# One decoder layer on one Trainium2 core: the last chunk's value and gate tiles taken by pairs of rows at the seam between feed-forward and mixer

## What is computed

```python
x = x + 0.5 * rmsnorm(swiglu_ffn(rmsnorm(x, ffn1_pre_g), ffn1_w_gu, ffn1_w_down), ffn1_post_g)
# mixer
u = rmsnorm(x, mix_pre_g) @ w_in
u_val, u_glu, u_x, u_gelu = jnp.split(u, [D_CONV, 2 * D_CONV, 2 * D_CONV + D_LRU], axis=-1)
g = u_val * sigmoid(u_glu)                       # "value" and "gate" of the conv branch
c = silu(rmsnorm(causal_dwconv([conv_buf | g], conv_w, conv_b), conv_norm_g))
yb = rg_lru(causal_dwconv([lconv_buf | u_x])) * gelu(u_gelu)
x = x + rmsnorm(concat(c, yb) @ w_out, mix_post_g)
# second feed-forward half step, gated per-layer embedding
```

## Time and profile before

| | |
|---|---|
| median of 3 runs | 2153.56 us (2152.64 to 2153.91) |
| profiled execution | 2149.13 us |
| its span, first to last instruction | 2147.0 us |
| mean granted TensorE clock | 0.99 |
| PE busy | 2084.6 us, 97% |
| DVE busy | 1189.7 us, 55% |
| ACT busy | 684.9 us, 32% |
| POOL busy | 70.0 us, 3% |

### The profile page before, as it was taken

How to read it: one execution, slowest core, us unless ns; L and a number is a source line. 1 busy time by engine, 2 the same in 40 slices (tenths; PEclk the granted TensorE clock), 3 DMA queues, 4 the chain that set the end, 5 groups by cost and what they waited for, 6 DMA issues and landing times. The chain is left out here.

```text
span 2147.0 us, 34634 instructions
## 1 busy us (share of the span) xinstructions
PE 2084.6 (97%) x13116; PEld 2071.4 (96%) x13116; DVE 1189.7 (55%) x2368; ACT 684.9 (32%) x1403; POOL 70.0 (3%) x109
## 2 busy tenths in 40 slices
PE   7999999999999998999989999999999999999998
PEld 7999999999999998999979999999999999999998
DVE  5643545344543578447765764354534454367877
ACT  4321222212122234216774542111221212123555
POOL 0000000000000001330000000000000000000000
PEclk9999999999999999999999999999999999999999
DMA  5170111011101100332121311011101110011212
GB/s 163 60 115 23 59 59 59 10 49 59 59 23 36 59 20 25 75 65 40 40 70 51 98 57 43 19 59 59 59 10 49 59 59 27 32 59 45 75 40 101
DMA packets 153277, 116.17 MB, mean 54 GB/s; under 512 B 72648, under 2 KB 143628, under 8 KB 153200
## 3 DMA queue, kind: packets, MB, share of 16 engines
q1 hardware_dynamic: 117728, 108.41, 16.2%
q10 hardware_dynamic: 33424, 5.67, 1.9%
q0 software_dynamic: 2048, 1.06, 0.3%
HBM read 105.96 MB, written 9.15 MB: 54 GB/s over the span
## 5 line engine op out<-in xcount | busy, mean ns | idle before, releaser
L845 PE MATMUL ps<-x_hi,w_lo 128*128 128x352 f32 x2688 | 885.9, 330 | 13.9 <-DVE x_lo L2093 8.1
L847 PE MATMUL ps<-x_hi,w_hi 128*128 128x352 f32 x2688 | 871.3, 324 | 0.0
L846 PE MATMUL ps<-x_lo,w_hi 128*128 128x352 f32 x2688 | 867.0, 323 | 0.0
L845 PEld LDWEIGHTS ps<-x_hi,w_lo 128*128 128x128 f32 x2688 | 507.5, 189 | 16.4 <-DVE x_lo L2093 7.8
L846 PEld LDWEIGHTS ps<-x_lo,w_hi 128*128 128x128 f32 x2688 | 510.9, 190 | 0.0
L847 PEld LDWEIGHTS ps<-x_hi,w_hi 128*128 128x128 f32 x2688 | 508.0, 189 | 0.0
L845 PE MATMUL ps<-a_hi,wd_lo 128*128 128x352 f32 x1104 | 360.0, 326 | 9.2 <-DVE a_lo L2149 7.3
L847 PE MATMUL ps<-a_hi,wd_hi 128*128 128x352 f32 x1104 | 358.7, 325 | 0.0
L846 PE MATMUL ps<-a_lo,wd_hi 128*128 128x352 f32 x1104 | 356.8, 323 | 0.0
L2200 DVE TENSOR_TENSOR acc<-ps,acc 128x352 f32<-128x352 f32 x480 | 249.7, 522 | 91.0 <-PE ps L847 82.9
L2132 DVE TENSOR_TENSOR tmp_u<-ps,rstd_pre 128x352 f32<-128x352 f32 x132 | 69.0, 524 | 341.5 <-PE ps L847 341.5
(11 more groups left out here) (226 smaller groups left out, 1597.7 us busy)
## 6 DMA issues: line engine op xcount, KB each, us to landing
raw<-in_ffn_w_gu_dram SPq DMA_DIRECT2D x88, 512.0 KB, 3.5
rawd<-in_ffn_w_down_dram SPq DMA_DIRECT2D x22, 1024.0 KB, 7.9
raw<-in_w_in_dram SPq DMA_DIRECT2D x16, 512.0 KB, 4.6
raw<-in_w_out_dram SPq DMA_DIRECT2D x16, 512.0 KB, 3.5
raw<-in_ple_w_gate_dram SPq DMA_DIRECT2D x16, 512.0 KB, 3.6
toeplitz<-rev ACTq DMA_DIRECT2D x8, 512.0 KB, 8.3
x_in<-in_x_prompt_dram SPq DMA_DIRECT2D x4, 512.0 KB, 10.1
toep_first<-toeplitz SPq DMA_DIRECT2D x32, 64.0 KB, 2.3
```

The source lines that it names most:

```text
L845: eng.matmul(dst, wl, xh, start=first, stop=False)
L846: eng.matmul(dst, wh, xl, start=False, stop=False)
L847: return eng.matmul(dst, wh, xh, start=False, stop=last)
```

## The change

All of it lies at the seam between the first feed-forward half and the mixer.

1. TensorE, chunk 2: in place of two groups of eight rows each, the four tiles go pair of rows by pair of rows (`vg_part`): for q = 0 to 3, wait for `x_lo` of pair q, rows 2q and 2q+1 of tiles 0 and 1, then of tiles 2 and 3. `norm_sum("pre2", 2)` stands behind the whole.
2. TensorE, norms: `norm_sum("pre2", 1)` and `norm_spread("pre2", 1)` move from rows 0 and 1 of chunk 2 to rows 5 and 7 of chunk 1; `norm_spread("pre2", 2)` moves from row 1 to row 3 of `in_unit(2)`'s first tile.
3. TensorE, weights: the four uses of `in_unit` (units 2, 3, 6, 7) wait for the first half of their weights at row 0 and for the second at row 4 of the first tile.
4. VectorE: the `x_lo` of pair q of chunk 2 comes before the `post1_pair` of pair q+1, with one short block between (`glu_mults(0)`, `values(1)`, `glu_gates(1)`); the adds of squares of chunk 2 are moved back behind; `split_wide(mix + 2)` comes before `glu_mults(1)`.
5. ScalarE: the mean of ("pre2", 1) comes before pair (2, 0), its spread before pair (2, 1); in pairs 2 and 3 of chunk 2 `x_hi` goes ahead, and the squares 4 to 7 are spread over the places behind, two of them behind `glu_batch(1)`.

```diff
-            def tile_product(dst, s, t, c, mid=None, xs=(x_hi, x_lo)):
+            def tile_product(dst, s, t, c, mid=None, xs=(x_hi, x_lo), halves=None):
                 for k in range(KT):
+                    if halves is not None and k % 4 == 0:
+                        eng.wait_ge(wide_lo, halves + k // 4 + 1)
...
+            def vg_part(c, ns, q):
+                eng.wait_ge(x_lo_done, PAIRS * c + q + 1)
+                for n in ns:
+                    at = RING["vg", c, n]
+                    dst = bank(at) if q == 0 else ps[:, at % BANKS, 0:C]
+                    for k in (2 * q, 2 * q + 1):
+                        wh, wl = wide(n // 2, k, n % 2)
+                        mm = passes(dst, wh, wl, x_hi[:, k, cols(c)], x_lo[:, k, cols(c)],
+                                    k == 0, k == KT - 1)
+                    if q == PAIRS - 1:
+                        mm.then_inc(psum_full, 1)
             def second_norms(k):
-                if k == 0:
+                if k == 5:
                     norm_sum("pre2", 1)
-                if k == 1:
+                if k == 7:
                     norm_spread("pre2", 1)
-            def third_norms(k):
-                if k == 4:
-                    norm_sum("pre2", 2)
...
-            vg_group(1, (0, 1, 2, 3))
-            vg_group(2, (0, 1), second_norms)
-            vg_group(2, (2, 3), third_norms)
+            vg_group(1, (0, 1, 2, 3), second_norms)
+            for q in range(PAIRS):
+                vg_part(2, (0, 1), q)
+                vg_part(2, (2, 3), q)
+            norm_sum("pre2", 2)
...
             def in_unit(u, behind=None, mid=None):
-                eng.wait_ge(wide_lo, 2 * (WIDE0["mix"] + u + 1))
...
-                                 mid and (lambda k: mid(n, k)))
+                                 mid and (lambda k: mid(n, k)),
+                                 halves=2 * (WIDE0["mix"] + u) if n == 0 else None)
...
-                if (n, k) == (0, 1):
+                if (n, k) == (0, 3):
                     norm_spread("pre2", 2)
```

ScalarE:

```diff
             pre2_pair(1, 3)
+            mean("pre2", 1)
             pre2_pair(2, 0)
-            mean("pre2", 1)
+            spread("pre2", 1)
             pre2_pair(2, 1)
-            spread("pre2", 1)
-            pre2_pair(2, 2)
+            pair_hi(2, 0, acc_tile, 2)
+            pre2_square(4)
+            pair_hi(2, 0, acc_tile, 3)
+            pre2_square(5)
             glu_batch(1)
-            pre2_pair(2, 3)
+            pre2_square(6)
+            pre2_square(7)
             split_wide(WIDE0["mix"] + 2)
```

VectorE:

```diff
-            post1_pair(2, 0)
+            post1_pair(2, 0, ())
             glu_mults(0)
-            post1_pair(2, 1)
-            post1_pair(2, 2)
+            pair_x_lo(2, 0, acc_tile, 0)
+            post1_pair(2, 1, ())
             values(1)
+            add_square(NORM["pre2", 2], 1)
+            pair_x_lo(2, 0, acc_tile, 1)
+            post1_pair(2, 2, ())
             glu_gates(1)
-            post1_pair(2, 3)
+            pair_x_lo(2, 0, acc_tile, 2)
+            post1_pair(2, 3, ())
+            add_square(NORM["pre2", 2], 2)
+            add_square(NORM["pre2", 2], 3)
+            pair_x_lo(2, 0, acc_tile, 3)
+            for m in range(4, KT):
+                add_square(NORM["pre2", 2], m)
+            split_wide(WIDE0["mix"] + 2)
             glu_mults(1)
-            split_wide(WIDE0["mix"] + 2)
             values(2)
```

More of the change, by code:

```diff
@@ L1440, in squares, with pair_hi @@
                     square(i, m, src(m), sem_, count0 + m + 1)
-            def apply_pair(name, c, x0, src, q):
-                i = NORM[name, c]
+            def pair_hi(c, x0, src, q):
                 eng.wait_ge(x_new, x0 + PAIRS * c + q + 1)
@@ L1448, in apply_pair @@
                                ).then_inc(x_hi_done, 1)
+            def apply_pair(name, c, x0, src, q):
+                pair_hi(c, x0, src, q)
                 for m in (2 * q, 2 * q + 1):
-                    square(i, m, src(c, m)[:, 0, :])
+                    square(NORM[name, c], m, src(c, m)[:, 0, :])
             def silu(f, i, c, h):
@@ L1629, in pre2_pair, with pre2_square @@
                 apply_pair("pre2", c, 0, acc_tile, q)
+            def pre2_square(m):
+                square(NORM["pre2", 2], m, acc_tile(2, m)[:, 0, :])
             for m in range(KT):
@@ L2089, in bank_last, with pair_x_lo @@
                 return bank(n)
-            def pair_low(pre, c, x0, src, p):
+            def pair_x_lo(c, x0, src, p):
                 eng.wait_ge(x_hi_done, x0 + PAIRS * c + p + 1)
@@ L2095, in pair_low @@
                                   ).then_inc(x_lo_done, 1)
+            def pair_low(pre, c, x0, src, p):
+                pair_x_lo(c, x0, src, p)
                 for k in (2 * p, 2 * p + 1):
```

## The result

| | before | after |
|---|---|---|
| median | 2153.73 us (2152.64 to 2155.23, 4 runs) | 2196.41 us (2193.12 to 2197.85, 4 runs) |
| ratio, 95% interval | | 1.0199 (1.0187 to 1.0211) |
| profiled execution, its span | 2149.13, 2147.0 us | 2197.85, 2195.8 us |
| mean granted TensorE clock | 0.990 | 0.965 |

I forecast 2145.5 us, 8.1 faster. It is 42.7 slower.

A forecast was written before the change was run, and what follows sets the result against it. TensorE, busy 97%, was taken as the bound, with 12.2 us lost at chunk 2 as ceiling; 9.88 won there, 8.85 after the grown matrix stall, less 0.8 for the clock, gave 8.1: 2145.5 us, range 2142.0 to 2149.2.

The forecast's parts named there:

- the chain through chunk 2: VectorE at chunk 2: x_lo of pairs 0 to 3 ends at 837.7, 843.06, 847.68, 852.38; the last was 855.42 before.
- the mended norm wait: TensorE at chunk 2: with chunk 1's norm moved, the spread doesn't wait and the 1.19 us stall by GpSimd's root goes.
- the new wait of `values(1)` on VectorE: VectorE, after pair (2, 1): `values(1)` waits 0.4 us for the spread root at 840.87, everything of chunk 2 queued behind.
- the wait at the last `x_lo`: TensorE before pair 3 of chunk 2: a wait of 0.88 us, products starting at 852.53.
- the new wait for `w_lo`: Start of `in_unit(2)`: TensorE waits 1.26 us for the first half of the weights and goes at 858.28.
- the `gate_raw` memset 8.85 sooner: VectorE, behind chunk 2's spread: the memset, then SP's loads and the convolution matrix, come 8.85 us sooner; TensorE 9.88.
- the pause grown to "about 2.05": TensorE's stall before the first convolution part, by the matrix DMA, grows from 1.11 to about 2.05 us.
- three signs of being wrong: Last `x_lo` of chunk 2 ending after 853.5, clock falling before 875, or `gate_raw` memset not moving by about 8.85.
- the price of that fall: Pause before the first convolution part: a clock fall would cost 1.6 us; half of it, 0.8, was taken.
- the row at 1015.36: Earlier trace: after a 2.02 us pause matmuls ran at the lower level some 3.6 us; taken as the fall's length.
- 0.134: Extra us each matmul takes at half clock: one starts each 0.1595 at full level, each 0.293 at 1.2 GHz.
- E: Rival: slower; waits between 24-matmul pieces in chunk 2 keep the clock at 1.2 GHz from 840 on, 2158 us; 3%.

The follow-up runs named there:

- the kernel with the spread put back: Changed kernel with norm_spread(pre2, 2) back from row 3 to row 1 of in_unit(2)'s first tile: 2141.59 us, ratio 0.9955.
- the kernel with wide matmuls in the midst: Changed kernel plus 24 wide matmuls between the second and third convolution tile: 2161.64, 2163.53, 2161.49, 2159.23, 2153.17 and 2146.52 us.
- the thinned kernel: Changed kernel without one of the two convolution matmuls of each step (product with the block before): 2127.71 and 2124.18 us.
- its lengthened form: The thinned kernel with two more gate_raw memsets on VectorE ahead of SP's loads, lengthening the pause: 2126.95 us (3 runs).

## Why the prediction was wrong

Right, by its own steps: the chain through chunk 2 (each of the four points within 0.2 us, above), the mended norm wait, the new wait of `values(1)` on VectorE (0.42, forecast 0.4), the wait at the last `x_lo` (0.63, forecast 0.88), the new wait for `w_lo` (1.11, forecast 1.26), the `gate_raw` memset 8.85 sooner (868.21 less the offset of 3.07, against 873.93: 8.79), the pause grown to "about 2.05" (2.19), the full clock from 840 to 875. The gain up to the first convolution step was 8.69 us, forecast 8.85. And the forecast named the place, this pause, as one at which the clock might fall. None of its three signs of being wrong came: the last `x_lo` ended at 852.47 with the offset taken off, the clock fell only at 877.1, the memset moved as forecast.

Wrong was one term of the sum, the price of that fall. I took 1.6 us from the row at 1015.36, and half of it; it was 51.6. The row was the wrong neighbour. Behind the pause at 1015.36 came only wide matmuls, 21 of them up to the next convolution step, and the clock was back at 1019.00. Behind mine came 64 rows with convolution steps, and I gave their fall the same length. The trace of before shows no low clock in mixed rows, as there they ran at 1.00; the fall should therefore have been bounded from both sides, by one short stretch (1.6 us) and by all 64 mixed rows. At my own 0.134 their 192 wide matmuls alone make 25.7 us, and at doubled spacing, 0.93 more for each row, it is 59.5. With the chance of the fall at a half, that alone would have made a range past 2170 and put a large chance on slower. In E I even priced the lower level "through pairs 0 to 3 and into `in_unit(2)`" at 2158, but asked for it by waits inside chunk 2, and gave it 3%, on the argument that the longest slow stretch seen was ten us. That stretch, too, had been ended by wide matmuls.

Nor is there an edge between 1.85 and 2.02 us, on which I put my pause. The two pauses of the earlier trace rows stand in other kernels of this study too, with the same matmuls behind them. The one of 2.02 kept the clock in the changed kernel, the one of 1.85 lost it in the kernel with the spread put back (PE timelines):

```profile
1061.98 0.43 PE L845 MATMUL ps_aux<-xc_hi,gw_lo 128*128 128x352 f32 x1 [2.02 <-DVE xc_lo L2627]
1062.25 0.32 PE L846 MATMUL ps_aux<-xc_lo,gw_hi 128*128 128x352 f32 x1
```
```profile
1113.83 0.43 PE L845 MATMUL ps<-y_hi,w_lo 128*128 128x352 f32 x1 [1.85 <-DVE w_lo L2067]
1114.10 0.41 PE L846 MATMUL ps<-y_lo,w_hi 128*128 128x352 f32 x1
1114.30 0.50 PE L847 MATMUL ps<-y_hi,w_hi 128*128 128x352 f32 x1
```

The Trainium skill, page "TensorE: Matmul & The Clock Gate", section "What's actually happening", says that activity releases the throttle. The measurement sets a limit to that: TensorE was busy 110 of 110 us at 0.50. In section "Seeing it yourself" the same page of the Trainium skill warns that the clock's records have been seen stuck low (at a quarter, not at a half as here) for over 50 us and should not be fully trusted; here the durations (0.49 for 0.32), the row spacing (1.73 for 0.93) and the device time all say the same as the record, so this low clock was real.

Not settled: by what chance a pause of a given length makes the clock fall. At 1.11 us it was 1 of 43 runs, at 1.28 none of 5, at 2.25 two of 4, at 2.61 three of 4, at 2.19 four of 4, at 2.06 (the kernel with wide matmuls in the midst) at least four of 6, at 3.81 two of 2. At 1.91 the profiled run of the thinned kernel kept it and at 3.52 that of its lengthened form lost it. These pauses are read from one profiled run of each kernel, so the other runs' may differ a little.

## What to carry to other kernels

Ahead of a long stretch whose matmuls are partly narrow, as here, price a pause of TensorE by the whole stretch at half clock, times the chance that the clock falls, and not by the pause. Look for what lies behind the next wait before winning a microsecond ahead of it; here an earlier DMA issue, or a few matmuls of no use in the gap, was worth 50 us. And when a change makes one side of a meeting point earlier by more than the other (here TensorE by 9.8 us, the memset that the matrix waits for by 8.8), move the other too.

## What the runs showed of the hardware

- One and the same instruction stream has two lasting speeds: 0.93 us for each mixed row when entered at 2.4 GHz, 1.73 us when entered at 1.2 GHz, the latter for 110 us with TensorE busy throughout.
- Plain wide matmuls bring the clock back in the midst of it (2.8 us after the first of the 24 added ones; at the end of the mixed rows 1.8 us after the first plain one), and with half of the narrow ones left out it came back within the mixed rows, by 885 us, 6 us behind the pause.
- Whether a pause near 2 us takes the clock away differs from run to run of the same program (two of four at 2.25 us, three of four at 2.61).
